# Twelve gathered U rows multiplied by GpSimd and summed by ScalarE while the gate matrix is built

## The reference

```
idx = e1 * N_KEYS + e2;  gate = softmax(best)
act = gelu(einsum('bqhkd,bqd->bqhk', expert_u[idx], xb))
out = einsum('bqhk,bqhkd->bqd', gate * act, expert_v[idx])
```

## Time and profile before

| | us |
|---|---|
| median of three runs | 1759.27 (1756.52 to 1762.42) |
| the profiled execution | 1760.75 |
| its span, first to last instruction | 1759.1 |
| PE busy | 1632.8 (93%) |
| VectorE busy | 1192.8 (68%) |
| GpSimd busy | 903.4 (51%) |
| ScalarE busy | 324.5 (18%) |

### The profile page before, as it was taken

How to read it: one execution, slowest core, us unless ns; L and a number is a source line. 1 busy time by engine, 2 the same in 40 slices (tenths; PEclk the granted TensorE clock), 3 DMA queues, 4 the chain that set the end, 5 groups by cost and what they waited for, 6 DMA issues and landing times.

```text
span 1759.1 us, 20536 instructions
## 1 busy us (share of the span) xinstructions
PE 1632.8 (93%) x6606; PEld 1166.5 (66%) x6606; DVE 1192.8 (68%) x2646; ACT 324.5 (18%) x751; POOL 903.4 (51%) x1129
## 2 busy tenths in 40 slices
PE   7989999998999888888799999999999999999996
PEld 6568876885777657777456666665666666666663
DVE  4377522887875678989866666666566666666766
ACT  4133311212333111178200000001000000000001
POOL 6976400686765466800564544444554454544443
PEclk9989999999999999999899999999999999999998
DMA  6312263446435986300799999999999999999997
GB/s 230 108 61 73 73 215 121 151 143 224 129 120 169 400 293 250 108 0 0 269 398 407 405 409 409 409 409 394 390 397 410 409 409 409 409 407 409 409 409 286
DMA packets 139100, 489.48 MB, mean 278 GB/s; under 512 B 16496, under 2 KB 17008, under 8 KB 138880
## 3 DMA queue, kind: packets, MB, share of 16 engines
q0 software_dynamic: 73728, 268.47, 39.2%
q1 hardware_dynamic: 65280, 219.85, 34.0%
HBM read 483.53 MB, written 4.72 MB: 278 GB/s over the span
## 4 chain that ended last, share of the span: by engine, by line
DMA 43%; PE 25%; DVE 13%; POOL 11%; issue 5%; ACT 3%; DVEq 0%; SPq 0%; POOLq 0%; ACTq 0%
DMA ring<-in_expert_v,chosen 25%; DMA ring<-in_expert_rows,chosen 14%; PE pair L697 7%; PE pair L709 4%; POOL ring L663 4%; DVE ring L1367 3%; PE pair L971 2%; DVE ring L1364 2%; PE pair L958 2%; DMA temp<-in_expert_v 2%; PE pair L887 2%; DVE temp L1577 2%; PE pair L743 1%; PE pair L789 1%; PE pair L766 1%
## 5 line engine op out<-in xcount | busy, mean ns | idle before, releaser
L958 PE MATMUL pair<-temp,hnT 128*128 128x512 f32 x984 | 448.3, 599 | 20.0 <-DVE hnT L1243 15.5
L663 POOL DMA_INDIRECT ring<-in_expert_rows,chosen x256 | 286.6, 1120 | 335.3 <-DVE ring L1364 296.2
L1367 DVE SCALAR_TENSOR_TENSOR ring<-ring,chosen 128x1024 f32<-128x1024 f32 x256 | 329.0, 1285 | 157.7 <-DMA ring<-in_expert_v,chosen 156.1
L949 PE MATMUL pair<-hnT,temp 128*128 128x256 f32 x1904 | 430.4, 379 | 0.0
L949 PEld LDWEIGHTS pair<-hnT,temp 128*128 128x128 f32 x1904 | 361.8, 190 | 100.0 <-issue 56.4
L1364 DVE SCALAR_TENSOR_TENSOR ring<-ring 128x1024 f32<-128x1024 f32 x256 | 318.2, 1255 | 137.9 <-DMA ring<-in_expert_rows,chosen 137.2
L663 POOL DMA_INDIRECT ring<-in_expert_v,chosen x256 | 260.0, 1016 | 265.0 <-DVE ring L1367 240.3
L958 PEld LDWEIGHTS pair<-temp,hnT 128*128 128x128 f32 x984 | 185.8, 192 | 216.0 <-issue 205.2
L1217 ACT ACTIVATE hnT<-pair 128x256 f32<-128x256 f32 x119 | 45.5, 384 | 804.2 <-PE pair L949 804.1
L697 PE MATMUL pair<-hnT,gate_all 128*128 128x256 f32 x656 | 152.1, 390 | 1.4 <-issue 1.4
L697 PEld LDWEIGHTS pair<-hnT,gate_all 128*128 128x128 f32 x656 | 126.9, 197 | 19.0 <-issue 1.7
(11 more groups left out here) (287 smaller groups left out, 2011.2 us busy)
## 6 DMA issues: line engine op xcount, KB each, us to landing
temp<-in_expert_v SPq DMA_DIRECT2D x128, 512.0 KB, 6.8
temp<-in_expert_u SPq DMA_DIRECT2D x119, 512.0 KB, 6.8
gate_all<-in_w_query SPq DMA_DIRECT2D x27, 512.0 KB, 3.6
ring<-in_w_g SPq DMA_DIRECT2D x16, 512.0 KB, 3.5
gate_all<-in_w_g SPq DMA_DIRECT2D x11, 512.0 KB, 3.5
gate_all<-in_expert_u SPq DMA_DIRECT2D x9, 512.0 KB, 3.5
ring<-in_w_u SPq DMA_DIRECT2D x8, 512.0 KB, 4.2
ring<-in_w_out SPq DMA_DIRECT2D x8, 512.0 KB, 4.5
```

Of the source, the lines that this page charges most:

```text
L663: pool.indirect_dma_start(out=gathered[:, g % SLOTS, :], out_offset=None, in_=(expert_rows, expert_v_rows)[part], in_offset=bass.IndirectO ...
L949: mm = pe.matmul(u_out[n % 2], u_in[:, n % 2, c * P:(c + 1) * P], hnT[:, c, FIRST[1]:L], start=(c == 0), stop=(c == DC - 1))
L958: mm = pe.matmul(pairs[i][:, b * 512:(b + 1) * 512], weighed[n][:, i * P:(i + 1) * P], v_in[:, n % 2, b * 512:(b + 1) * 512], start=False, ...
L1367: dve.scalar_tensor_tensor(out=fin, in0=slot, scalar=wsel[:, at:at + 1], in1=fin, op0=ALU.mult, op1=ALU.add).then_inc(row_done, 1)
```

## The change

Twelve U rows, 70 to 81, leave the loop. When GpSimd has finished its part of the second half's lists it takes these rows one by one: it multiplies the slot with `xrow` in place, waits for that, adds the right half of the slot to the left half in place (128 x 512), signals `row_halved`, and issues the next gather, which as before waits until `row_done` frees the slot. ScalarE sums the left half into the column of `wsel` (a copy to the right half of the slot with an accumulator, `row_total`) after groups 4, 9, ... 59 of the building stage and increments `row_done`. Its loop over the groups is written out in full. VectorE waits for 82 rows before the expert loop and starts there with row 82; `LATE` is 430, and `rows_by` shifts accordingly.

```diff
--- before.py
+++ after.py
@@ -99,12 +99,13 @@
 
 ROWS_BEFORE_LOOP, ROWS_PER_STEP, ROWS_PER_MERGE, ROWS_BEFORE_QUERY = 6, 1, 2, 32
 EARLY = ROWS_BEFORE_LOOP + NT * ROWS_PER_STEP + DC * ROWS_PER_MERGE + ROWS_BEFORE_QUERY
-LATE = ROWS - EARLY
+POOL_ROWS = 12
+LATE = ROWS - EARLY - POOL_ROWS
 AHEAD = 9
 
 
 def rows_by(n):
-    return EARLY + (n + 1) * LATE // P
+    return EARLY + POOL_ROWS + (n + 1) * LATE // P
 
 
 def step_of(rows):
@@ -336,7 +337,7 @@
         numbers_ready = sem("numbers_ready")
         oh2_marked, oh1_ready, oh2_ready, onehot_free, gmat_free = (
             sem("oh2_marked"), sem("oh1_ready"), sem("oh2_ready"), sem("onehot_free"), sem("gmat_free"))
-        sel_gelu, row_done = sem("sel_gelu"), sem("row_done")
+        sel_gelu, row_done, row_halved = sem("sel_gelu"), sem("row_done"), sem("row_halved")
         row_landed = [sem(f"row_landed{i}") for i in range(SLOTS)]
         u_landed = [sem(f"u_landed{i}") for i in range(2)]
         v_landed = [sem(f"v_landed{i}") for i in range(2)]
@@ -676,6 +677,13 @@
                 gather_to(SLOTS + ROWS_BEFORE_LOOP + i * ROWS_PER_STEP)
             gather_to(SLOTS + EARLY)
             find_lists(1)
+            for g in range(EARLY, EARLY + POOL_ROWS):
+                slot = gathered[:, g % SLOTS, :]
+                pool.wait_ge(row_landed[g % SLOTS], 16 * (g // SLOTS + 1))
+                pool.wait_ge(row_done, EARLY)
+                chain(pool.tensor_tensor(slot, slot, xrow, ALU.mult))
+                pool.tensor_tensor(slot[:, 0:D // 2], slot[:, 0:D // 2], slot[:, D // 2:D], ALU.add).then_inc(row_halved, 1)
+                gather_to(g + SLOTS)
             gather_to(ROWS)
 
         @block.tensor
@@ -1194,17 +1202,21 @@
                               pairs[2 + b // 2][:, (b % 2) * 512:(b % 2 + 1) * 512].rearrange("p (t e) -> p e t", t=4),
                               ACT.Copy).then_inc(gmat_free, 1)
 
+            def row_total(r):
+                g = EARLY + r
+                slot = gathered[:, g % SLOTS, :]
+                ac.wait_ge(row_halved, r + 1)
+                ac.activation(slot[:, D // 2:D], slot[:, 0:D // 2], ACT.Copy, accum_out=wsel[:, g:g + 1]).then_inc(row_done, 1)
+
+            quads = HALF // 4
             widen(0, 0)
             widen(1, 1)
-            with ac.Fori(0, HALF // 16 - 1) as it:
-                for b in range(4):
-                    widen(it * 4 + b + 2, (b + 2) % 4)
-                    read_gates(it * 4 + b, b, bass.ds(it * 16 + b * 4, 4))
-            for b in range(4):
-                g = HALF // 4 - 4 + b
-                if b < 2:
-                    widen(g + 2, b + 2)
-                read_gates(g, b, slice(4 * g, 4 * g + 4))
+            for g in range(quads):
+                if g + 2 < quads:
+                    widen(g + 2, (g + 2) % 4)
+                read_gates(g, g % 4, slice(4 * g, 4 * g + 4))
+                if g % 5 == 4 and g // 5 < POOL_ROWS:
+                    row_total(g // 5)
 
             def select_gelu(i):
                 ac.wait_ge(row_done, (2 * i + 1) * PICKS)
@@ -1589,6 +1601,8 @@
                                          op1=ALU.mult).then_inc(out_ready, 1)
 
             dve.wait_ge(gmat_free, 4 + HALF // 4)
+            dve.wait_ge(row_done, EARLY + POOL_ROWS)
+            emitted[0] = EARLY + POOL_ROWS
             for n in range(P):
                 if n >= AHEAD:
                     dve.wait_ge(gelu_done, n + 1)
```

## The result

The changed kernel takes 1781.66 us in the median of four runs (1779.59 to 1786.41), against 1758.36 (1756.52 to 1762.42) for the kernel before beside it: a ratio of 1.0122, 95% interval 1.0102 to 1.0142, 23.3 us slower. The prediction was 1785, 1766 to 1806. The profiled execution after took 1786.41 us (span 1784.8), the slowest of its four, 4.7 above their median; 2.6 us of that lie ahead of the change, as GpSimd's last list instruction starts at 755.24 instead of 752.61.

The account below looks back on a forecast made before the run. VectorE was taken to bound the building stage, DMA the expert loop, with PE close behind. Stage 33 + 2 + 2 + 1 = +38 and loop -12 gave net +26 us, 1785 us in the median, range 1766 to 1806.

Parts of the forecast that it names:

- both forms: Building stage: marks (two SBUF inputs) and tensor_scalars (two elements at a time) should both wait for GpSimd.
- rows 2 to 11: Building stage: ten rows on GpSimd each hold VectorE up 3.3 us, 33 us together.
- gathers in the stage: Building stage: twelve gathers issued there lengthen tensor_scalars by 0.19 us each, 2 us, bounds 0 and 11.
- rows 0 and 1: Around the building stage's start: delayed VectorE list operations and overlap with the first marks cost 2 us, bounds 0 and 5.
- PE's clock: Building stage: PE idles longer and runs slower for a few microseconds after a stall; 1 us, bounds 0 and 15.
- loop: Expert loop: 12 fewer gathered rows relieve DMA until PE becomes the bound; gain 12 us, between 6 and 15.4.
- the discount of 0.18: Building stage: a GpSimd operation takes 0.18 us less from VectorE than recorded, making a row 3.27 instead of 3.63 us.
- A: Building stage: only marks waits for GpSimd, 2.1 us a row; net +13, 1772 us; chance 0.08.
- B: Building stage: VectorE doesn't wait for GpSimd; stage +0 to +1, loop -12, 1747 us; chance 0.07.
- C: Building stage: PE's lowered clock makes it PE-bound, +53 instead of +38, 1800 us, up to 1812; chance 0.08.
- D: Expert loop: PE already bounds it, so nothing comes back; +38 alone gives 1797 us; chance 0.07.
- the long marks: Building stage, sign of the forecast: marks with maxima above 2 us, 10 to 20 of them, only beside GpSimd.

Follow-up runs that it names:

- one-at-a-time run: Changed kernel with each tensor_scalar also writing an accumulator and adding the gate instead of multiplying by it: 1788.66 us (1 run).
- products only: Kernel before, all 442 rows kept in the loop, plus ten pairs of GpSimd additions in the building stage, no gather between them: 1790.82 us, ratio 1.0175.
- gather apart: Changed kernel, but GpSimd waits until the gather it just issued has landed before multiplying the next row: 1778.33 us, ratio 1.0100.
- odd width: Changed kernel with the tensor_scalars writing 127 columns instead of 128: 1779.84 us (1 run).
- no products: Changed kernel without GpSimd's multiply and fold per row; handshakes, gathers and ScalarE totals stay: 1745.63 us, ratio 0.9919.
- VectorE's twelve rows: Kernel before with the same twelve rows moved to VectorE, four before the building stage and eight inside it: 1752.29 us, ratio 0.9957.
- no fold: Changed kernel with GpSimd's multiply only; ScalarE sums all 1024 elements: 1772.64 us, ratio 1.0076.
- the four rows in the gap: Kernel before with four rows moved into VectorE's idle time before the building stage: 1751.22 us, ratio 0.9952; repeated 1753.08 us, 0.9952.

## Why the prediction was right

The mechanism held: VectorE waits for GpSimd's operations in both forms, and bounds the stage. The size was close, and closer than the terms deserve. In the stage the rows cost 3.7 more than forecast and the three small terms 4.0 less, which is luck; the loop gave back 2.5 more. And +25.7 between the profiles meets the forecast of +26 only by the 2.6 us that lie ahead of the change: the change itself made 23.1 in the profiles and 23.3 in the medians.

| term | predicted | measured |
|---|---|---|
| rows 2 to 11 | 10 x 3.3 = 33 | 10 x 3.67 = 36.7 |
| gathers in the stage | 2 | 0 alone, in the 3.67 where a multiply follows |
| rows 0 and 1 | 2 | 1.2 (0.96 of it in the stage) |
| PE's clock | 1 | 0 |
| stage | +38 | +37.7 |
| loop | -12 (-6 to -15.4) | -14.5 |
| the change in all | +26 | +23.1 (profiles), +23.3 (medians) |

- The order of bounds was right: every delay of VectorE lengthened the stage by itself, since VectorE has no gap there. The inference from a tensor_scalar of 0.55 us instead of 0.30 to the 128-element ones, which the trace of before never showed beside GpSimd, was right too, and the one-at-a-time run shows the two forms apart.
- The size per row. For a multiply and a fold alone 3.27 was estimated, from 0.55 lost of 0.73 recorded. The GpSimd product under which VectorE's began there is another one, from 517.99, and is recorded as 0.94 in the trace of before, so the discount of 0.18 is taken against a record that isn't that of the product concerned. 3.12 and 3.15 were measured where no gather stands ahead. The Trainium skill, SBUF — State Buffer, section Who interferes with whom, has the shared pair locked for the whole instruction, which for ten rows would be 36.3 us of recorded time; where the pair stands alone the measured 31 us lie below it. The 36.7 of the changed kernel come near that figure only because the gather ahead adds 0.5 us per row. That 0.5 was the mis-sized term: the prediction had 0.2 for a gather, taken from a tensor_scalar of 0.94 instead of 0.75.
- PE's clock. The stage's granted clock fell from 1.00 to 0.85 and cost nothing. PE came back from each stall slower, in the row shown with 40 matmul records in 6.57 us, that is 1.31 a group of eight instead of 1.13. That is still under VectorE's 1.36. After the first stall it was 7.05 us, 1.41 a group, and the next stall took up what PE was behind. VectorE's 37.7 us of added time are the whole growth of the stage. The forecast's 2.2 us a group doesn't follow from its row: four records in 1.19 make 2.4 for eight.
- The loop. PE's waits on the product fell by 13.2 and those on V rose by 1.9; the busy share of PE in an undisturbed stretch is 100.00 of 100 us, as before. With the products only, at 442 rows, the gain is -2.6; with 12 rows gone it was -14.5 to -19.3 in seven kernels, one profile each (-14.5 changed kernel, -16.3 one at a time, -16.4 gather apart, -16.6 odd width, -17.1 no products, -18.7 VectorE's twelve rows, -19.3 no fold). The reason given for 12 rather than 15.4, that PE becomes the bound, was not needed: the gain came near the bytes' 15.4 and in six of the seven passed it, by up to 3.9, which is more than bytes explain. With the four rows in the gap this is the part left open.
- The rivals. A (only marks waits): tensor_scalars were held up to 3136 ns. Its price of 2.1 us a row doesn't follow from the 1.03 us given for it, which would leave 1.1 under the multiply and 0.1 under the fold; in the one-at-a-time run, which is this rival made true, a row cost 2.42. B (VectorE doesn't wait): +37.7. C (PE's clock): 0.85, at no cost. D (loop gives nothing): -14.5. Each had a sign in the profile that could be read at once. Of the forecast's own signs the long marks failed to show, and the clock's 0.85 is lower than "1.00 or little under it".
- A reading. The 0.66 us by which GpSimd's product is said to end after VectorE's counts from VectorE's accumulator read at 519.94; from the end of the row shown it is 0.58. Nothing in the sum rests on it.

## What to carry to other kernels

An idle engine is free only if it doesn't hold up the one that bounds the stage: GpSimd's tensor operations on SBUF took 3.67 us of VectorE's time for a row that VectorE does in 1.15. Before an offload to an engine that the bounding one waits for, divide the borrowed engine's recorded time by the bounding engine's own time for the work; above one, the offload costs that stage more than doing the work there. Look instead for a gap of the bounding engine itself: here 5.56 us between two of its phases held four rows, and that version beats both kernels (0.9952).

## What the runs showed of the hardware

- A GpSimd multiply queued directly behind a gather's issue holds VectorE about 0.5 us longer than the same pair after a wait (3.60 to 3.88 against 3.12 to 3.15 us). An issue with nothing behind it cost VectorE nothing.
- Without a gather ahead, a pair costs VectorE 3.12 to 3.15 us, and the records of multiply and fold are longer in the median: 2.56 and 1.26 (gather apart), 2.41 and 1.26 (products only). Part of that is GpSimd's own wait, since the multiply takes 2.35 in the changed kernel; against 2.35 and 1.26 about half a microsecond is left.
- A tensor_scalar of 127 elements runs at the speed of 128 (334 ns) and waits in the same way. The Trainium skill, VectorE: DVE Perf Modes, section What auto-detection actually checks, asks that the outermost sizes of source and destination be both even or equal; by that rule 127 on both sides qualifies, and this run agrees.
- The tensor_scalar that writes an accumulator takes 397 ns and was never held. The Trainium skill, SBUF — State Buffer, section Who interferes with whom, leaves this form out of those that take the shared ports, and the trace agrees.
